# Hybrid decoder layer on one core: the last two row tiles share one attention-times-values visit, and output products move between scores and transposes

## The chip, the cores and the metric

The kernel runs on one core of a Trainium2 chip. The metric is the device time of one execution in microseconds, here the median of three runs. It is written directly against the engines: each engine has its own program, and semaphores order them.

## What is computed

The reference is one decoder layer over 512 tokens of width 1024, in float32:

```
h = x @ w_in                       # one projection, split into q,k,v,gates,indexer,latents
o_a = dsa(qa, ka, va, iq, ik, iw) * silu(ga)    # branch A: each query attends to its top-128 keys, 8 heads of 64
o_b = mla(c_q, c_kv, k_rope, ...) * silu(gb)    # branch B: causal latent attention, 8 heads of 64 (+32 rotary)
out = concat(o_a, o_b) @ w_out
x   = layernorm(alpha * x + out) * ln_g + ln_b
```

## The kernel before, in words

Tokens are cut into four row tiles of 128 (TT = 4), which are taken in the order 3, 2, 1, 0 (`ORDER`), so that the causal length falls: a query tile has 4, 3, 2 and then 1 key tiles. "Tile 0" below is the first that is taken and "tile 3" the last, with one key tile.

After the projections TensorE runs a pipeline over 64 units u. Units 0 to 31 are branch A, units 32 to 63 are branch B: eight heads for each row tile, so tile 2 of branch B is units 48 to 55 and tile 3 is units 56 to 63. For one unit of branch B:

- TensorE makes the scores (`scores`, L1335) into one of two PSUM banks.
- VectorE masks them into `probs` and takes the row maximum (`mask_unit`, L996).
- ScalarE takes the exponential (`exp_unit`, L752).
- VectorE divides by the row sum, two units later (`normalise_b`, L1033 and L1035).
- TensorE transposes the result three units later (`transposes`, L1368), and ScalarE copies it out of PSUM (`copy_probsT`, L771).
- Once per row tile, five units after its last head, TensorE multiplies all eight heads with the values (`outputs`, L1406; called a visit below). The result is gated by VectorE (`gate_obT`, L1044).

The gated result of a row tile is `oT`, in halves: half 0 is branch A (k = 0 to 3), half 1 is branch B (k = 4 to 7). Each half is split for precision: ScalarE rounds it to a high part (`copy_oT_hi`, L782), and VectorE or GpSimd subtracts that to get the low part (`oT_low`, L386). The output projection (`out_products`, L1445) takes high times high, high times low weights, and low times high: 48 products of 128x512 for a row tile (the last tile has three column pieces of 512, 256 and 256 instead of two of 512, so 24 products of 512 and 48 of 256). They are handed out a few per unit as filler. VectorE then does the layer norm: `ln_residual` (L1055 and L1060) reads the output bank and thereby frees it, then `ln_stats`, `ln_centre` (L1071), `ln_scale` (L1078). GpSimd takes the root of the variance (L614). SyncE stores.

Every engine works through its own list in the order in which the code is written. The lists of ScalarE and VectorE that matter here, for unit u:

```
ScalarE: copy_probsT(u-3); copy_oT_hi(i-1, 0) if u is 48+4 or 56+4 ...; exp_unit(u); ...
VectorE: normalise_b(u-2); mask_unit(u); oT_low(V, i-1, 0) and gate_obT(i-1) if u%8 == 4; layer norm pieces
```

The layer norm pieces of tile 0 stand at units 53 to 57 and those of tile 1 at units 61 to 65. The output banks of tiles 0 to 2 are the same two, so the first product of a tile waits (`out_ps_read`) for the `ln_residual` of the tile before.

Of the kernel before, what the change touches and what calls it, by code (L numbers as in the profile page):

```python
# [6 lines left out]
P = 128  # L7
# [19 lines left out]
def build(nc, x, xT, positions, pos_row, freqs, w_in, q_norm_g, w_uq, kv_norm_g, w_ukv, w_out, ln_g, ln_b, out):  # L27
# [98 lines left out]
    for u in range(NU):  # L126
        slots.append(u)
        for i in range(TT):
            if u == G_AFTER[i]:
                slots.append((i,))  # L130
    OUT_AT = [NU_A + HEADS * (i + 1) + OT_AT + 2 for i in range(TT)]

    PIECES = [[slice(0, BANK), slice(BANK, D_MODEL)]] * (TT - 1) + [[slice(0, BANK), slice(BANK, BANK + BANK // 2),
# [56 lines left out]
    qaT = sb("qaT", 162, [P, A_HEADS, SEQ], f32r)  # L190
    oT1 = sb("oT1", 24, [P, 2, KT, P], f32r)
    probsT_b = [sb(f"probsT_b{j}", kib, [P, BANK]) for j, kib in enumerate((162, 164, 166, 168, 170, 172, 174, 176, 88, 90, 196, 198))]

    probs = sb("probs", 16, [P, NPROBS, BANK])
    trig_tmp = sb("trig_tmp", 178, [P, 2, TT * FREQ_B])
# [36 lines left out]
    with ExitStack() as ctx:  # L232
# [125 lines left out]
        def copy_free(eng, u):  # L358

            if u < NU_A:  # L360
                if last_user(u) is not None:
                    eng.wait_ge(pv_done, HEADS * (last_user(u) // HEADS + 1))
                return probsT[u][:, :]
            if u >= NU_A + len(probsT_b):
                eng.wait_ge(pv_done, HEADS * ((u - len(probsT_b)) // HEADS + 1))
            return probsT_b[(u - NU_A) % len(probsT_b)][:, 0:unit(u)[3]]

        def oT_src(i, b):

# [10 lines left out]
        def oT_low(eng, i, b):  # L380

            dst = (oT0, oT1)[i % 2]
            eng.wait_ge(oT_hi_ready, 2 * i + b + 1)
            if i + b > 0:
                eng.wait_ge(oT_lo_ready, 2 * i + b)
            eng.tensor_tensor(dst[:, 1, 4 * b:4 * b + 4, :], oT_src(i, b), dst[:, 0, 4 * b:4 * b + 4, :],  # L386
                              ALU.subtract).then_inc(oT_lo_ready, 1)

        def out_steps(i):


            halves = ((0, KT // 2), (KT // 2, KT))
            blocks = [(b, h) for h in halves for b in range(len(PIECES[i]))] if i < TT - 1 else \
                     [(b, h) for b in range(len(PIECES[i])) for h in halves]
            return [(b, k, j) for b, (k0, k1) in blocks for low in (False, True)
                    for k in range(k0, k1) for j in ((2,) if low else (0, 1))]

# [103 lines left out]
        def _(pool):  # L501
# [112 lines left out]
                pool.tensor_tensor(rstd, aggr[:, 2:3], minus_half[:, 0:1], ALU.pow).then_inc(rstd_ready, 1)  # L614


            for i in range(TT):
                if i < TT - 1:
                    oT_low(pool, i, 1)
                if i == 1:  # L620
                    root(0)
            root(1)
            root(2)
            root(3)


        @block.scalar
        def _(act):
# [161 lines left out]
            for u in range(NU + T_LAG):  # L790
                for w in turned_at(u):
                    if not by_dve(w):
                        copy_probsT(w)
                i, j = divmod(u - NU_A, HEADS)
                if 1 < i < TT and j == OT_AT:
                    copy_oT_hi(i - 1, 0)
                if 2 <= u < NU:
                    exp_unit(u)
                if u in VB_AT:
                    copy_vb(VB_AT.index(u))  # L800
                if u == O_FIRST:
                    copy_oT_hi(0, 0)
                for t in range(TT):
                    if u == TURN_AT[t]:
                        turn_gate(t)
                if 0 < i < TT and j == OT_AT + 1:
                    copy_oT_hi(i - 1, 1)
            copy_oT_hi(TT - 1, 0)
            copy_oT_hi(TT - 1, 1)


# [1 line left out]
        def _(dve):  # L813
# [274 lines left out]
            for u in range(NU):  # L1088
                if u - NORM_LAG >= NU_A:
                    normalise_b(u - NORM_LAG)  # L1090
                if u >= 2:
                    mask_unit(u)
                for w in turned_at(u):
                    if by_dve(w):
                        copy_probsT(w)
                v, j = divmod(u, HEADS)
                i = v - TT
                if u in (BLOCK_UNITS + 2, NU_A + 2):
                    row_sums_a(u // BLOCK_UNITS - 1)
                for t in range(TT):  # L1100
                    if u == GATE_AT[t]:
                        gate_oaT(t)
                for n in range(TT):
                    if u == PET_AT[n]:
                        qpe_blocks(n)
                if 1 < i and j == OT_AT:
                    oT_low(V, i - 1, 0)
                if 0 < i and j == OT_AT:
                    gate_obT(i - 1)
                for t in range(TT - 2):  # L1110
                    for at_u, take in ln_schedule(t):
                        if at_u == u:
                            take()
# [23 lines left out]
        def _(pe):  # L1137
# [233 lines left out]
            def outputs(u):  # L1371
# [21 lines left out]
                                    ins.then_inc(pv_done, 1)  # L1393
                    return

                i = v - TT
                if h < HEADS - 1:
                    return
                pe.wait_ge(*((o_ps_read, TURN_RANK.index(A_RANK[i]) + 1) if i < 2 else (ob_ps_read, i - 1)))
                for w in range(u - HEADS + 1, u, 2):  # L1400
                    for a in range(2):
                        wait_copied(pe, w + a)
                    h = unit(w)[2]
                    for j in range(m + 1):
                        for a in range(2):
                            ins = mm(ps_o[A_DIM * a:A_DIM * (a + 1), i % 2, h // 2 * P:(h // 2 + 1) * P],  # L1406
                                     vb[:, j, (h + a) * V_DIM:(h + a + 1) * V_DIM],
                                     probsT_b[(w + a - NU_A) % len(probsT_b)][:, j * P:(j + 1) * P], start=(j == 0), stop=(j == m))
                            if j == m:
                                ins.then_inc(pv_done, 1)  # L1410

# [9 lines left out]
            def out_products(i, a, z):  # L1421
# [3 lines left out]
                for n in range(a, z):  # L1425
                    b, k, j = steps[n]
                    first, final = n == steps.index((b, 0, 0)), n == steps.index((b, KT - 1, 2))
                    cols = PIECES[i][b]
                    half, wcols = cols.start // BANK, slice(cols.start % BANK, cols.start % BANK + cols.stop - cols.start)
                    if b == 0 and j in (0, 2) and k in (0, KT // 2):  # L1430
                        pe.wait_ge((oT_hi_ready, None, oT_lo_ready)[j], 2 * i + 1 + (k > 0))
# [20 lines left out]
            for u in range(NU + PV_LAG):  # L1452
                if 2 <= u < NU:
                    scores(u)
                for w in turned_at(u):
                    transposes(w)
                if u in VB_AT:
# [7 lines left out]
                i, j = divmod(u - NU_A, HEADS)  # L1465
# [3 lines left out]
                if 0 <= u - A_HALF_AT < 8:  # L1469
                    out_products(0, 3 * (u - A_HALF_AT), 3 * (u - A_HALF_AT + 1))  # L1470
                if 0 <= u - OUT_AT[0] - 2 < 6:
                    out_products(0, 3 * KT + 4 * (u - OUT_AT[0] - 2), 3 * KT + 4 * (u - OUT_AT[0] - 1))
                for t in range(1, TT - 1):
                    if 0 <= u - OUT_AT[t] < HEADS:
                        out_products(t, per * (u - OUT_AT[t]), per * (u - OUT_AT[t] + 1))
# [66 lines left out]
```

## Time and profile before

| | |
|---|---|
| median of 3 runs | 291.01 us (290.87 to 291.7) |
| profiled execution, its own time | 291.71 us |
| its span in the trace | 289.9 us |
| TensorE busy | 281.6 us, 97% of the span |
| VectorE busy | 234.3 us, 81% |
| ScalarE busy | 148.4 us, 51% |
| GpSimd busy | 168.2 us, 58% |
| TensorE granted clock over the span | 0.995 |

A matmul that follows another starts before the modelled end of the first, so the time that one costs is the distance between starts and not its own duration. Times inside the trace are counted from the start of the span.

### The profile page before, as it was taken

Reading aid. Unit: us, or ns where it says so; the run is one execution under the profiler, and the core shown is the slowest. Engines: PE = TensorE matmul, PEld = TensorE weight load, DVE = VectorE, ACT = ScalarE, POOL = GpSimd, SP = SyncE. Lnnn points to the kernel's source line nnn. Section 1 sums busy time; section 2 is a strip of 40 time slices with the busy share of each in tenths; the row PEclk is TensorE's granted clock in tenths of the full one; section 3 lists DMA queues with packets and bytes.
Section 4 is the critical chain, followed back from the end, with each engine's and each line's share of the span. In section 5 each row is a group of like instructions: output and inputs, shape, how many; then the busy total and the mean of one; then the engine's idle time right before and its main releaser. Section 6 shows DMA issues by size and latency. Waiting matters only on the chain.

```text
span 289.9 us, 5157 instructions
## 1 busy us (share of the span) xinstructions
PE 281.6 (97%) x1696; PEld 234.8 (81%) x1696; DVE 234.3 (81%) x536; ACT 148.4 (51%) x351; POOL 168.2 (58%) x174
## 2 busy tenths in 40 slices
PE   8999999999999999999999999999999999999990
PEld 8999987778888888888888887885778788887890
DVE  2799498889999999999984788668894759786755
ACT  4765353585433367224188696677773744432000
POOL 5698956333089999999946999632990102011101
PEclk9999999999999999999999999999999999999997
DMA  7966662222604297221238667507800000400412
GB/s 229 350 195 187 179 176 72 75 72 67 153 4 142 72 222 216 72 72 38 72 102 196 222 144 235 123 2 280 300 2 2 0 3 1 145 2 5 142 72 72
DMA packets 20074, 34.20 MB, mean 118 GB/s; under 512 B 6640, under 2 KB 9200, under 8 KB 19792
## 3 DMA queue, kind: packets, MB, share of 16 engines
q1 hardware_dynamic: 19616, 33.71, 39.3%
q8 instruction: 14, 0.23, 0.3%
q10 hardware_dynamic: 432, 0.16, 0.3%
q14 instruction: 12, 0.10, 0.1%
HBM read 26.52 MB, written 2.10 MB: 99 GB/s over the span
## 4 chain that ended last, share of the span: by engine, by line
PE 96%; DVE 2%; issue 1%; DVEq 0%; POOL 0%; POOLq 0%
PE ps L1143 52%; PE ps L1445 16%; PE ps L1368 6%; PE ps L1335 6%; PE ps L1406 3%; PE ps L1389 3%; PE ps L1158 2%; PE ps L1325 2%; PE ps L1328 2%; PE ps L1278 1%; PE ps L1252 1%; PE ps L1418 1%; DVE y_last L1071 1%; PE ps L1261 0%; PE ps L1235 0%
## 5 line engine op out<-in xcount | busy, mean ns | idle before, releaser
L533 POOL TENSOR_TENSOR w_lo<-w_raw,w_hi 128x512 fp32r<-128x512 f32 (+3 forms) x62 | 82.8, 1355 | 26.7 <-ACT w_hi L645 26.0
L645 ACT ACTIVATE w_hi<-w_raw 128x512 fp32r<-128x512 f32 (+3 forms) x62 | 36.0, 589 | 57.7 <-PE ps L1143 55.7
L752 ACT ACTIVATE probs<-probs,small 128x512 f32<-128x512 f32 (+3 forms) x64 | 35.7, 558 | 18.6 <-DVE small L996 18.3
L1143 PE MATMUL ps<-w_hi,x_lo 128*128 128x512 f32 (+2 forms) x128 | 45.0, 356 | 0.0
L1445 PE MATMUL ps<-wo_hi,oT 128*128 128x512 f32 (+1 forms) x144 | 44.9, 383 | 0.0
L1143 PE MATMUL ps<-w_lo,x_hi 128*128 128x512 f32 (+2 forms) x128 | 44.9, 356 | 0.0
L1143 PE MATMUL ps<-x_hi,w_hi 128*128 128x512 f32 x96 | 38.1, 396 | 0.0
L1143 PE MATMUL ps<-x_hi,w_lo 128*128 128x512 f32 x96 | 37.4, 390 | 0.0
L1143 PE MATMUL ps<-x_lo,w_hi 128*128 128x512 f32 x96 | 37.4, 390 | 0.0
L1143 PE MATMUL ps<-w_hi,x_hi 128*128 128x512 f32 (+1 forms) x92 | 34.8, 378 | 0.0
L1445 PEld LDWEIGHTS ps<-wo_hi,oT 128*128 128x128 f32 x144 | 25.9, 189 | 4.0 <-issue 0.5
L1368 PE MATMUL ps<-ident,probs 128*128 128x128 f32 x160 | 28.6, 276 | 0.3
L1368 PEld LDWEIGHTS ps<-ident,probs 128*128 128x128 f32 x160 | 19.5, 140 | 10.8 <-issue 6.2
L1143 PEld LDWEIGHTS ps<-w_hi,x_lo 128*128 128x128 f32 x128 | 24.1, 188 | 2.5
L1143 PEld LDWEIGHTS ps<-w_lo,x_hi 128*128 128x128 f32 x128 | 24.1, 188 | 2.5
L953 DVE MATCH_REPLACE8 score<-small,score 128x256 f32<-128x256 f32 (+2 forms) x48 | 25.5, 541 | 0.0
L996 DVE CUSTOM_DVE_ANT_0 probs<-ps,causal 128x128 f32<-128x128 f32 (+3 forms) x40 | 17.8, 446 | 9.4 <-PE ps L1335 8.0
L386 POOL TENSOR_TENSOR oT<-gate,oT 128x512 fp32r<-128x512 f32 x4 | 5.1, 1284 | 34.2 <-ACT oT L782 34.2
L950 DVE MAX8 small<-score 128x8 f32<-128x256 f32 (+2 forms) x48 | 23.5, 544 | 0.0
L1335 PE MATMUL ps<-kbT,qbT 96*128 96x512 f32 (+3 forms) x64 | 22.6, 434 | 0.0
L1143 PEld LDWEIGHTS ps<-x_hi,w_hi 128*128 128x128 f32 x96 | 18.0, 188 | 4.9 <-ACT w_hi L645 0.7
L771 ACT ACTIVATE probsT_b<-ps 128x512 f32<-128x512 f32 (+3 forms) x32 | 13.8, 432 | 15.8 <-PE ps L1368 15.6
(163 smaller groups left out, 606.5 us busy)
## 6 DMA issues: line engine op xcount, KB each, us to landing
w_raw<-in_w_in SPq DMA_DIRECT2D x20, 512.0 KB, 3.7
kaT_swap<-kaT SPq DMA_DIRECT2D x8, 256.0 KB, 3.8
w_raw<-in_w_out SPq DMA_DIRECT2D x4, 512.0 KB, 4.2
wo_early<-in_w_out SPq DMA_DIRECT2D x4, 512.0 KB, 3.7
wo_raw_b<-in_w_out SPq DMA_DIRECT2D x4, 512.0 KB, 5.2
x_res<-in_x SPq DMA_DIRECT2D x4, 512.0 KB, 7.0
x_raw<-in_xT SPq DMA_DIRECT2D x3, 512.0 KB, 7.3
out_y<-y SPq DMA_DIRECT2D x6, 256.0 KB, 2.1
```

The costliest lines, as they stand in the source:

```text
L533: pool.tensor_tensor(w_lo[:, s, 0:n], w_raw[:, s, 0:n], w_hi[:, s, 0:n], ALU.subtract).then_inc(w_lo_ready, 1)
L645: act.activation(dst, w_raw[:, s, 0:n], ACT.Copy).then_inc(w_hi_ready, 1)
L752: act.activation(probs[:, u % NPROBS, 0:N], probs[:, u % NPROBS, 0:N], ACT.Exp, bias=neg_max[:, u % 8:u % 8 + 1], scale=-1.0, accum_out=ro ...
L771: act.activation(dst, ps_pT[:, slot_of[u] % 2, 0:N], ACT.Copy).then_inc(probsT_copied, 1)
L950: step(V.max(top8[:, 8 * j:8 * j + 8], sc))
L953: step(V.match_replace(out=sc, in_to_replace=top8[:, 8 * j:8 * j + 8], in_values=sc, imm_value=TAKEN))
L996: V.tensor_tensor_reduce(out=probs[:, u % NPROBS, 0:N], in0=ps_s[:, u % 2, 0:N], in1=bias, scale=-scale, scalar=3.0e38, op0=ALU.add, op1=A ...
L1143: ins = mm(dst, a, b, start=start and j == 0, stop=stop and j == len(pairs) - 1)
L1335: ins = mm(ps_s[:, b, 0:N], qbT[:, h, t], kbT[:, h, 0:N], start=True, stop=True)
L1368: ins = nc.tensor.transpose(bank[:, j * P:(j + 1) * P], probs[:, u % NPROBS, j * P:(j + 1) * P], ident[:, :])
L1389: ins = mm(oa_bank(v)[A_DIM * a:A_DIM * (a + 1), h // 2 * P:(h // 2 + 1) * P], va[:, j, (h + a) * A_DIM:(h + a + 1) * A_DIM], probsT[w + 2 ...
L1445: ins = mm(out_ps(i, b), oT[i % 2][:, o, k, :], w[:, wcols], start=first, stop=final)
```

## The change

Three things are done together.

1. Inside each unit TensorE's output products stand between the scores and the transposes; before, they stood after the transposes, the visit and the gate transposes.
2. The visit of tile 2 (units 48 to 55, made at unit 60) is put off to unit 68 and made with that of tile 3. Their transposed probabilities get their own buffers (`short_b`), in space that is free by then.
3. The output products of tile 2 in units 62 to 67 are now four per unit and only its first half (24 products). After the common visit come 12 products of tile 3 (half 0, first piece), then tile 2's other 24, then tile 3's remaining 60. Tile 3's products go by halves first and pieces second. The gating, the high part and the low part of tile 2's half 1 move to the end of the lists of VectorE and ScalarE, and its low part from GpSimd to VectorE.

```diff
+    SPLIT_ORDER = [(0, 0), (0, 1), (1, 0), (1, 1), (2, 0), (3, 0), (2, 1), (3, 1)]
...
+    short_b = [sb(f"short_b{n}", kib, [P, unit(NU - 2 * HEADS + n)[3]]) for n, kib in
+               enumerate([170 + n for n in range(HEADS)] + [88 + n / 2 for n in range(HEADS)])]
...
-            blocks = [(b, h) for h in halves for b in range(len(PIECES[i]))] if i < TT - 1 else \
-                     [(b, h) for b in range(len(PIECES[i])) for h in halves]
+            blocks = [(b, h) for h in halves for b in range(len(PIECES[i]))]
...
             # GpSimd
+            for i in range(TT - 2):
+                oT_low(pool, i, 1)
             for i in range(TT):
-                if i < TT - 1:
-                    oT_low(pool, i, 1)
-                if i == 1:
-                    root(0)
-            root(1)
...
             # ScalarE
-                if 0 < i < TT and j == OT_AT + 1:
+                if 0 < i < TT - 1 and j == OT_AT + 1:
                     copy_oT_hi(i - 1, 1)
-            copy_oT_hi(TT - 1, 0)
+                if u == NU:
+                    copy_oT_hi(TT - 1, 0)
+            copy_oT_hi(TT - 2, 1)
             copy_oT_hi(TT - 1, 1)
...
             # VectorE
-                if 0 < i and j == OT_AT:
+                if 0 < i < TT - 1 and j == OT_AT:
                     gate_obT(i - 1)
...
-            gate_obT(TT - 1)
-            oT_low(V, TT - 1, 1)
+            for t in range(TT - 2, TT):
+                gate_obT(t)
+            for t in range(TT - 2, TT):
+                oT_low(V, t, 1)
...
             # TensorE, outputs
-                if h < HEADS - 1:
+                if h < HEADS - 1 or v == NPASS - 2:
                     return
...
             # TensorE, the loop over units
                 if 2 <= u < NU:
                     scores(u)
+                if 0 <= u - A_HALF_AT < 8:
+                    out_products(0, 3 * (u - A_HALF_AT), 3 * (u - A_HALF_AT + 1))
+                if 0 <= u - OUT_AT[0] - 2 < 6:
+                    out_products(0, 3 * KT + 4 * (u - OUT_AT[0] - 2), 3 * KT + 4 * (u - OUT_AT[0] - 1))
+                if 0 <= u - OUT_AT[1] < HEADS:
+                    out_products(1, per * (u - OUT_AT[1]), per * (u - OUT_AT[1] + 1))
+                if 0 <= u - OUT_AT[2] < 6:
+                    out_products(2, 4 * (u - OUT_AT[2]), 4 * (u - OUT_AT[2] + 1))
                 for w in turned_at(u):
                     transposes(w)
...
-            done = per * (NU + PV_LAG - OUT_AT[TT - 2])
-            out_products(TT - 2, done, NSTEP)
-            out_products(TT - 1, 0, 3 * KT * len(PIECES[TT - 1]))
+            last_first, last_all = 3 * KT // 2, 3 * KT * len(PIECES[TT - 1])
+            out_products(TT - 1, 0, last_first)
+            out_products(TT - 2, NSTEP // 2, NSTEP)
+            out_products(TT - 1, last_first, last_all)
```

TensorE's list at units 61 and 62, before. L1335 is `scores`, L1368 `transposes`, L1445 `out_products`; oT_97 belongs to tiles 1 and 3, oT_68 to tiles 0 and 2:

```order
L1335 MATMUL ps<-kbT,qbT 128x128
L1368 MATMUL ps<-ident,probs 128x128
L1445 MATMUL ps<-wo_hi,oT_97 128x512
L1445 MATMUL ps<-wo_lo_b,oT_97 128x512
L1445 MATMUL ps<-wo_hi,oT_97 128x512 x4
L1335 MATMUL ps<-kbT,qbT 128x128
L1368 MATMUL ps<-ident,probs 128x128
L1445 MATMUL ps<-wo_hi,oT_68 128x512
L1445 MATMUL ps<-wo_lo_a,oT_68 128x512
```

The same place in the changed kernel (L1349 is `scores`, L1382 `transposes`, L1461 `out_products`):

```order
L1349 MATMUL ps<-kbT,qbT 128x128
L1461 MATMUL ps<-wo_hi,oT_97 128x512
L1461 MATMUL ps<-wo_lo_b,oT_97 128x512
L1461 MATMUL ps<-wo_hi,oT_97 128x512 x4
L1382 MATMUL ps<-ident,probs 128x128
L1349 MATMUL ps<-kbT,qbT 128x128
L1461 MATMUL ps<-wo_hi,oT_68 128x512
L1461 MATMUL ps<-wo_lo_a,oT_68 128x512
```

The transpose of a unit now stands behind all its products, and the first product of tile 2 directly behind the scores of unit 62.

ScalarE's list at the end, before. L752 is the exponential, L771 the copy of a transposed unit, L782 the high part of an oT half:

```order
L771 ACTIVATE probsT_b_99<-ps 128x128
L782 ACTIVATE oT_68<-gate 128x512
L752 ACTIVATE probs,small<-probs,small 128x128
L771 ACTIVATE probsT_b_100<-ps 128x128
L752 ACTIVATE probs,small<-probs,small 128x128
L782 ACTIVATE oT_68<-gate 128x512
L771 ACTIVATE probsT_b_101<-ps 128x128
```

The same place in the changed kernel (L781 the copy, L792 the high part, L762 the exponential):

```order
L781 ACTIVATE short_b_119<-ps 128x128
L792 ACTIVATE oT_68<-gate 128x512
L762 ACTIVATE probs,small<-probs,small 128x128
L781 ACTIVATE short_b_120<-ps 128x128
L762 ACTIVATE probs,small<-probs,small 128x128
L781 ACTIVATE short_b_121<-ps 128x128
```

The high part of tile 2's half 0 (the first oT_68) still stands behind the copy of unit 57's transpose. The high part of its half 1 has left this place.

## Rows read from the trace of the kernel before

**Rows 1.** The page: busy time by engine, and the ending chain by engine.

```profile
PE 281.6 (97%) x1696; PEld 234.8 (81%) x1696; DVE 234.3 (81%) x536; ACT 148.4 (51%) x351; POOL 168.2 (58%) x174
...
PE 96%; DVE 2%; issue 1%; DVEq 0%; POOL 0%; POOLq 0%
```

**Rows 2.** The chain that ended last: start, us, what.

```profile
268.78 14.15 PE ps L1445 x84
```

**Rows 3.** Timeline, TensorE, unit 41: start us, us, engine, line, operation.

```profile
211.75 0.81 PE L1335 MATMUL ps<-kbT,qbT 96*128 96x384 f32 x2
212.53 0.63 PE L1368 MATMUL ps<-ident,probs 128*128 128x128 f32 x4
```

**Rows 4.** Timeline, TensorE, units 58 to 62.

```profile
248.74 0.39 PE L1335 MATMUL ps<-kbT,qbT 96*128 96x128 f32 x2
249.16 0.41 PE L1368 MATMUL ps<-ident,probs 128*128 128x128 f32 x2
...
252.52 0.38 PE L1335 MATMUL ps<-kbT,qbT 96*128 96x128 f32 x2
252.74 0.27 PE L1368 MATMUL ps<-ident,probs 128*128 128x128 f32 x1
252.95 1.97 PE L1406 MATMUL ps<-probsT_b,vb 128*64 128x128 f32 x32
...
256.33 0.39 PE L1335 MATMUL ps<-kbT,qbT 96*128 96x128 f32 x2
...
258.05 0.39 PE L1335 MATMUL ps<-kbT,qbT 96*128 96x128 f32 x2
```

**Rows 5.** Timeline, ScalarE, unit 60.

```profile
253.05 0.28 ACT L771 ACTIVATE probsT_b<-ps 128x128 f32<-128x128 f32 x1 [1.00 <-PE ps L1368]
253.23 0.62 ACT L782 ACTIVATE oT<-gate 128x512 fp32r<-128x512 f32 x1
```

**Rows 6.** Timeline, VectorE, units 60 to 63.

```profile
253.88 0.69 DVE L386 TENSOR_TENSOR oT<-gate,oT 128x512 fp32r<-128x512 f32 x1 [0.64 <-ACT oT L782]
...
256.97 0.68 DVE L1055 SCALAR_TENSOR_TENSOR y<-x_res,ps 128x512 f32<-128x512 f32 x1
...
258.30 0.15 DVE L1033 RECIPROCAL small<-small 128x1 f32<-128x1 f32 x1
258.48 1.07 DVE L1035 TENSOR_SCALAR probs<-probs,small 128x128 f32<-128x128 f32 x1
...
261.19 0.28 DVE L1035 TENSOR_SCALAR probs<-probs,small 128x128 f32<-128x128 f32 x1
261.39 0.28 DVE L996 CUSTOM_DVE_ANT_0 probs<-ps,causal 128x128 f32<-128x128 f32 x1
261.60 0.08 DVE L996 DVE_READ_ACCUMULATOR2_ANT small<- 128x1 f32 x1
...
262.57 0.16 DVE L1033 RECIPROCAL small<-small 128x1 f32<-128x1 f32 x1
```

**Rows 7.** Timeline, TensorE, unit 64.

```profile
261.62 0.30 PE L1368 MATMUL ps<-ident,probs 128*128 128x128 f32 x1
```

**Rows 8.** Timeline, GpSimd, around unit 62.

```profile
258.19 1.29 POOL L386 TENSOR_TENSOR oT<-gate,oT 128x512 fp32r<-128x512 f32 x1 [11.26 <-ACT oT L782]
```

**Rows 9.** Timeline, VectorE, units 52 and 53.

```profile
238.35 0.69 DVE L1044 TENSOR_TENSOR gate<-ps,gate 128x512 f32<-128x512 f32 x1 [1.18 <-PE ps L1406]
...
239.15 0.35 DVE L1035 TENSOR_SCALAR probs<-probs,small 128x256 f32<-128x256 f32 x1
239.87 0.42 DVE L996 CUSTOM_DVE_ANT_0 probs<-ps,causal 128x256 f32<-128x256 f32 x1 [0.37 <-PE ps L1335]
...
240.22 0.68 DVE L1055 SCALAR_TENSOR_TENSOR y<-x_res,ps 128x512 f32<-128x512 f32 x1
```

**Rows 10.** Timeline, TensorE, the two products that follow the scores of unit 1.

```profile
162.77 0.45 PE L1143 MATMUL ps<-latT_hi,w_hi 128*128 128x512 f32 x1
163.06 0.39 PE L1143 MATMUL ps<-latT_lo,w_hi 128*128 128x512 f32 x1
```

More of the change, by code:

```diff
@@ L363, in copy_free, with probsT_of @@
                 return probsT[u][:, :]
-            if u >= NU_A + len(probsT_b):
+            if u >= NU - 2 * HEADS:
+                eng.wait_ge(pv_done, HEADS * (u // HEADS - 1))
+            elif u >= NU_A + len(probsT_b):
                 eng.wait_ge(pv_done, HEADS * ((u - len(probsT_b)) // HEADS + 1))
-            return probsT_b[(u - NU_A) % len(probsT_b)][:, 0:unit(u)[3]]
+            return probsT_of(u)
+        def probsT_of(u):
+            n = u - (NU - 2 * HEADS)
+            return short_b[n][:, :] if n >= 0 else probsT_b[(u - NU_A) % len(probsT_b)][:, 0:unit(u)[3]]
         def oT_src(i, b):
@@ L382, in oT_low @@
             dst = (oT0, oT1)[i % 2]
-            eng.wait_ge(oT_hi_ready, 2 * i + b + 1)
-            if i + b > 0:
-                eng.wait_ge(oT_lo_ready, 2 * i + b)
+            n = SPLIT_ORDER.index((i, b))
+            eng.wait_ge(oT_hi_ready, n + 1)
+            if n > 0:
+                eng.wait_ge(oT_lo_ready, n)
             eng.tensor_tensor(dst[:, 1, 4 * b:4 * b + 4, :], oT_src(i, b), dst[:, 0, 4 * b:4 * b + 4, :],
@@ L614, in root @@
                 pool.tensor_tensor(rstd, aggr[:, 2:3], minus_half[:, 0:1], ALU.pow).then_inc(rstd_ready, 1)
+            for i in range(TT - 2):
+                oT_low(pool, i, 1)
             for i in range(TT):
-                if i < TT - 1:
-                    oT_low(pool, i, 1)
-                if i == 1:
-                    root(0)
-            root(1)
-            root(2)
-            root(3)
+                root(i)
         @block.scalar
@@ L1394, in outputs @@
                     return
-                i = v - TT
-                if h < HEADS - 1:
+                if h < HEADS - 1 or v == NPASS - 2:
                     return
-                pe.wait_ge(*((o_ps_read, TURN_RANK.index(A_RANK[i]) + 1) if i < 2 else (ob_ps_read, i - 1)))
-                for w in range(u - HEADS + 1, u, 2):
+                for w in range(u - (2 * HEADS if v == NPASS - 1 else HEADS) + 1, u, 2):
+                    v, m, h, N = unit(w)
+                    i = v - TT
+                    if h == 0:
+                        pe.wait_ge(*((o_ps_read, TURN_RANK.index(A_RANK[i]) + 1) if i < 2 else (ob_ps_read, i - 1)))
                     for a in range(2):
                         wait_copied(pe, w + a)
-                    h = unit(w)[2]
                     for j in range(m + 1):
@@ L1407, in outputs @@
                                      vb[:, j, (h + a) * V_DIM:(h + a + 1) * V_DIM],
-                                     probsT_b[(w + a - NU_A) % len(probsT_b)][:, j * P:(j + 1) * P], start=(j == 0), stop=(j == m))
+                                     probsT_of(w + a)[:, j * P:(j + 1) * P], start=(j == 0), stop=(j == m))
                             if j == m:
@@ L1430, in out_products @@
                     if b == 0 and j in (0, 2) and k in (0, KT // 2):
-                        pe.wait_ge((oT_hi_ready, None, oT_lo_ready)[j], 2 * i + 1 + (k > 0))
+                        pe.wait_ge((oT_hi_ready, None, oT_lo_ready)[j], SPLIT_ORDER.index((i, int(k > 0))) + 1)
                     if i == 0 and n in (0, 3 * KT):
@@ L1464, in _ @@
                     outputs(u - PV_LAG)
-                i, j = divmod(u - NU_A, HEADS)
                 for t in range(1, TT):
@@ L1468, in _ @@
                         gate_transposes(t)
[L1469 to L1475, printed above, removed]
-            done = per * (NU + PV_LAG - OUT_AT[TT - 2])
-            out_products(TT - 2, done, NSTEP)
-            out_products(TT - 1, 0, 3 * KT * len(PIECES[TT - 1]))
+            last_first, last_all = 3 * KT // 2, 3 * KT * len(PIECES[TT - 1])
+            out_products(TT - 1, 0, last_first)
+            out_products(TT - 2, NSTEP // 2, NSTEP)
+            out_products(TT - 1, last_first, last_all)
 NWARM = 9
```

## The prediction

> **What bounds the kernel now.** I read the page first, then the chain that ended last, then the timelines of the last 80 us engine by engine. TensorE is busy 97% of the span and is 96% of the chain [rows 1]. Behind the last visit it runs 84 products without a gap, to 282.93 [rows 2]; the span ends 7.0 us later with the layer norm of the last tile and its store. So nothing gets shorter unless TensorE does less, waits less, or that tail changes. The change removes no product. Its gain can only come from TensorE's waits in units 40 to 68, and any new wait there is paid in full, because behind it there is no slack until the end.
>
> How a wait is seen: the distance from one start to the next against what the work takes. The scores of one key tile take 0.22 us (252.52 to 252.74), and a unit with one key tile and six products takes 1.72 (256.33 to 258.05) [rows 4]. So six products with one transpose take 1.50; a transpose is 0.11 of that and a product 0.23. In unit 58 the transposes start 0.42 after the scores instead of 0.22 [rows 4], and in unit 41, with three key tiles, 0.78 after them instead of 0.66 [rows 3]: VectorE had not finished the division.
>
> **Output products ahead of the transposes: the gain.** In each unit a transpose now gets 0.7 to 1.4 us more before it can be late. Unit 58 saves 0.20 and unit 41 0.12. Two more units (40 and 56) show smaller excesses of the same kind, for which I estimate the mean of these two rows, 0.16 each at most; half of that is my value, so 0.5 us together, between 0.32 and 0.64. In unit 64 the transpose starts at 261.62 [rows 7] where two units of 1.72 behind 258.05 would put it at 261.49: 0.13 of wait, which goes or is replaced (below). Gain so far 0.6.
>
> **The common visit.** Unit 60 lasts 3.81 and a unit without a visit 1.72, so the visit costs 2.09 for products whose own group lasts 1.97 [rows 4]. The products remain; one entry and one exit go. The bounds are 0.1 and 0.3 (the 0.21 between transpose and visit instead of 0.11, and as much again at the exit); I take 0.15.
>
> **What is queued behind the later transposes: the loss.** ScalarE's list has, for unit 60: copy of transpose 57, high part of tile 2's half 0, exponential. Before, transpose 57 started at 252.74, its copy at 253.05, the high part at 253.23, and VectorE's low part at 253.88 [rows 4 to 6], so 1.14 behind the transpose. In the changed kernel the transpose stands behind six products, and these steps come later with it. VectorE's next instruction after the mask of unit 60 is that low part. It idles there some 2 us, although the input of the high part has been ready since branch A. Behind the low part wait, in this order: division of unit 59, mask 61, `ln_residual` of tile 1's first piece, and it is this last one that frees the bank for tile 2's first product.
>
> Call X the start of transpose 57. On VectorE:
> - the low part starts at X+1.14. A gating of the same form plus a reciprocal takes 0.80 (238.35 to 239.15) [rows 9], less 0.18 for the reciprocal (258.30 to 258.48) [rows 6]: 0.62;
> - a division of one key tile takes 0.18 + 0.20 (261.19 to 261.39), about 0.39, and a mask 0.21 (261.39 to 261.60) [rows 6];
> - so `ln_residual` starts at X+2.35, lasts 0.68 [rows 6] and reaches TensorE 0.12 later, at X+3.15. The 0.12 is the way from a division to a transpose (0.15 from 261.47 to 261.62, of which TensorE's load is a part) [rows 6, 7].
>
> On TensorE without a wait: transpose 0.11, unit 61 with 1.72, scores of unit 62 with 0.22: X+2.05. Before, the first product of tile 2 stood behind the transpose too and the residual at 256.97 was over by 257.65, while the scores came at 258.05 [rows 4, 6]: it had 0.6 us to spare. Now TensorE waits **1.1 us**.
>
> From there units 62 to 66 have four products, not six: 1.26 with scores, 1.04 without. TensorE reaches transpose 61 at X+6.4. VectorE: residual and statistics take 1.33 (256.97 to 258.30), then division 60, mask 62, another 1.33, division 61. This ends at X+2.35+1.33+0.60+1.33+0.39 = X+6.0: in time. Then mask 63, 0.21, and aggregate and centring, 0.97 (261.60 to 262.57) [rows 6], and division 62 ends at X+7.65, at TensorE X+7.8. Transpose 62 could start at X+7.5: **0.3 us** more of wait. Transpose 63 is in time.
>
> Here a neighbour matters. The division of unit 60 took 1.07 instead of 0.28 while GpSimd's low part of 1.29 us ran [rows 6, 8]. The change moves this to the end of VectorE's list, and I count division 60 at 0.39. If it stayed slow, 0.8 more would fall on VectorE's stretch, and some 0.4 on transpose 61. The Trainium skill (SBUF — State Buffer, Who interferes with whom) says that VectorE and GpSimd share one pair of ports under an exclusive lock; by that rule the slow division goes with its neighbour, and the trace agrees (1.07 beside, 0.28 apart).
>
> The same wait exists one tile earlier, smaller. Tile 1's first product in unit 54 needs tile 0's residual, which stands in unit 53 behind the gating at 238.35. Gating and reciprocal bring the division to 239.15, this gives way after 0.27 (0.35 less the overlap of 0.08), mask 0.35 (239.87 to 240.22), residual 0.68, signal 0.12 [rows 9]: 2.22 behind the gating. TensorE leaves the visit 0.14 before the gating starts and, by the prices above, needs 0.44 for scores, 0.92 for four products, 0.25 for two transposes and 0.44 for scores: 2.05, so 1.91 behind the gating. It waits **0.3**, where before the transposes and four products between visit and scores covered it.
>
> **A boundary that the trace hardly shows.** Scores now precede a product. After the scores of unit 1 two products lie 0.29 apart instead of 0.23 [rows 10]: at most 0.06 for each of 24 units, 1.4 us. Against that, transposes no longer precede products. Unit 61 shows no loss at that boundary (1.72 = 0.22 + 0.11 + 6 x 0.23). I take nothing, since the second pass of scores is as long as a transpose, and keep 1.4 for the upper end.
>
> **The last stretch.** GpSimd's roots no longer stand behind a low part, which nobody waits for, and SyncE's list is the same. Behind the common visit, 12 products of tile 3 (2.7 us) and the visit's last third (1 us) cover the gating (0.69), the high part (0.62) and the low part (0.69) of tile 2's half 1. VectorE has tile 2's layer norm, about 5.5 us, after tile 2's last product at +8.2; tile 3's first piece is complete at +13.8 and its second 1.44 before the last. Residual and statistics of that piece take 0.9. So the tail of 7.0 us is unchanged; if this cover failed it would cost up to 0.5.
>
> The Trainium skill (TensorE: Matmul & The Clock Gate, Architectural detail) states that ScalarE and VectorE work strictly first in, first out. By it the high part cannot pass the copy that waits, which is what this forecast needs. The row agrees in order (253.05, then 253.23), but no run here has yet shown it with the input waiting. If ScalarE could pass it, the 1.1 would vanish, as in the second rival.
>
> **Sum.** +1.1 +0.3 +0.3 -0.6 -0.15 = +0.95, taken as +0.9. The profiled execution took 291.71 for a span of 289.9, that is 1.8 outside it, and would give 292.6; it lies 0.7 above the median of 291.01, to which I add the same 0.9: **291.9 us**.
>
> **Rivals.**
> - *Waits as above (49 in 100):* 291.9, own range 291.2 to 292.6. It falls on both sides of the bound.
> - *The waits are small (16 in 100):* only 0.3 to 0.5 at tile 2's first product, since some step of the VectorE chain is quicker: 291.0 to 291.2, no change.
> - *The cover is complete (14 in 100):* this is the other side. If the residual of tile 1 is done by X+2.05, none of the three waits appears and the gains of 0.6 and 0.15 stay, up to 0.9 with their upper bounds: 290.1, faster. It decides at 1.1 us in the VectorE chain between low part and residual. For it speaks that VectorE idles 2 us there; against it, that the idle time is ahead of the chain and not in it.
> - *The boundary costs (21 in 100):* half to all of 1.4 on top of 0.9: 292.6 to 293.3, slower. For it the one row with 0.29, against it that there the weights differ.
>
> **How the numbers follow.** A measurement tells this kernel from no change at about 0.3%, 0.9 us (290.14 and 291.88). Faster: the third case, 0.14. Same: the second and half of the first, 0.16 + 0.24 = 0.40. Slower: the other half and the fourth, 0.46. The range goes down into the third case, to 290.3, and up into the fourth, to 292.9.
>
> **What would show it.** In the changed trace: transposes of units 41, 56 and 58 without excess; one visit of 48 products; VectorE idle some 2 us before the low part in unit 60; TensorE's first product of tile 2 about 1.1 late behind the scores of unit 62 and the first of tile 1 0.3 late in unit 54; transpose 62 late by 0.3; the tail of 7.0 unchanged. Wrong would be: no gap at those two products (then faster), gaps of more than 0.02 behind every score (then slower), or a wait of tile 2's half 1 behind the visit.

## The result, and the profile after

The changed kernel takes 292.05 us (median of 11 runs, 291.48 to 292.45) against 291.10 for the kernel before (11 runs beside it, 290.87 to 291.70). The ratio is 1.0026, 95% interval 1.0017 to 1.0036: slower by 0.76 us, between 0.5 and 1.05. The two medians lie further apart, 0.95, but inside that interval. The forecast was 291.9, 0.9 more than before.

The page of the changed kernel: its span, the busy time by engine as in [rows 1], and the row of the output products:

```profile
span 290.3 us, 5157 instructions
PE 279.9 (96%) x1696; PEld 233.3 (80%) x1696; DVE 231.9 (80%) x537; ACT 148.6 (51%) x351; POOL 167.3 (58%) x173
...
L1461 PE MATMUL ps<-wo_hi,oT 128*128 128x512 f32 (+1 forms) x144 | 46.8, 398 | 1.1 <-DVE y L1067 1.0
```

TensorE has 1.7 us less busy time. The last row has what takes its place: the output products (L1461) had idle time of 1.1 us before them, and 1.0 of it ended with VectorE's residual (L1067). That idle time was 0.0 before.

Spans also differ at their beginnings, where the kernels are the same. So I measure the part that the change touches by itself: from the first scores of unit 40, the first with three key tiles, to the last residual of the last tile. The kernel before (timelines of TensorE and VectorE):

```profile
209.88 0.81 PE L1335 MATMUL ps<-kbT,qbT 96*128 96x384 f32 x2
...
282.95 0.42 DVE L1055 SCALAR_TENSOR_TENSOR y_last<-x_res,ps 128x256 f32<-128x256 f32 x1 [1.99 <-PE ps L1445]
```

The changed kernel (timeline of TensorE; its last residual, at 283.31, is shown further down):

```profile
209.62 0.81 PE L1349 MATMUL ps<-kbT,qbT 96*128 96x384 f32 x2
```

Before, the stretch takes 73.07 us; in the changed kernel it takes 73.69, or 0.62 more.

TensorE in the changed kernel, units 60 to 65 (timeline; start us, us, engine, line, operation, idle time before it):

```profile
253.55 0.27 PE L1382 MATMUL ps<-ident,probs 128*128 128x128 f32 x1
253.66 0.38 PE L1349 MATMUL ps<-kbT,qbT 96*128 96x128 f32 x2
253.80 0.48 PE L1461 MATMUL ps<-wo_hi,oT 128*128 128x512 f32 x1
254.12 0.40 PE L1461 MATMUL ps<-wo_lo_b,oT 128*128 128x512 f32 x1
...
255.38 0.39 PE L1349 MATMUL ps<-kbT,qbT 96*128 96x128 f32 x2
256.73 0.47 PE L1461 MATMUL ps<-wo_hi,oT 128*128 128x512 f32 x1 [0.96 <-DVE y L1067]
257.04 0.39 PE L1461 MATMUL ps<-wo_lo_a,oT 128*128 128x512 f32 x1
...
258.99 0.27 PE L1382 MATMUL ps<-ident,probs 128*128 128x128 f32 x1
...
260.03 0.27 PE L1382 MATMUL ps<-ident,probs 128*128 128x128 f32 x1
...
261.34 0.30 PE L1382 MATMUL ps<-ident,probs 128*128 128x128 f32 x1
...
263.53 2.84 PE L1422 MATMUL ps<-short_b,vb 128*64 128x128 f32 x48
```

Unit 61 takes 1.72 (253.66 to 255.38), as before [rows 4]: a product behind scores costs nothing extra. From the start of the scores to that of the second product behind them is 0.46 in unit 61 (253.66 to 254.12) and 1.66 in unit 62 (255.38 to 257.04): tile 2's first product has waited 1.20. The trace puts a product's start early where it follows scores without a wait, so I measure such waits to the second product. Two transposes with four products between them are 1.04 apart when nothing waits (258.99 to 260.03); transpose 62 follows after 1.31, 0.27 late. The visit is one, of 48 products.

ScalarE's timeline of the changed kernel at the same place:

```profile
253.86 0.28 ACT L781 ACTIVATE short_b<-ps 128x128 f32<-128x128 f32 x1 [1.05 <-PE ps L1382]
254.03 0.62 ACT L792 ACTIVATE oT<-gate 128x512 fp32r<-128x512 f32 x1
254.56 0.39 ACT L762 ACTIVATE probs<-probs,small 128x128 f32<-128x128 f32 x1
```

VectorE's timeline of the changed kernel:

```profile
252.37 0.29 DVE L1008 CUSTOM_DVE_ANT_0 probs<-ps,causal 128x128 f32<-128x128 f32 x1 [0.65 <-PE ps L1349]
...
254.69 0.69 DVE L401 TENSOR_TENSOR oT<-gate,oT 128x512 fp32r<-128x512 f32 x1 [2.02 <-ACT oT L792]
255.30 0.15 DVE L1045 RECIPROCAL small<-small 128x1 f32<-128x1 f32 x1
...
255.90 0.68 DVE L1067 SCALAR_TENSOR_TENSOR y<-x_res,ps 128x512 f32<-128x512 f32 x1
```

ScalarE stood idle for 1.05 at the copy of transpose 57, although the high part behind it reads a tile that branch A had finished long before; VectorE stood idle for 2.02 at the low part. With X = 253.55, the start of transpose 57, the low part starts at X+1.14 and the residual at X+2.35, the two numbers of the prediction.

The chain that ended last in the changed kernel leaves TensorE at this one place of the stretch (start, us, what): it runs through the high part, the low part and the residual to tile 2's first products.

```profile
254.03 0.63 ACT oT L792
254.69 0.69 DVE oT L401
255.99 0.61 DVE y L1067
256.73 1.16 PE ps L1461 x4
```

One tile earlier, in unit 54, the same on a smaller scale (TensorE's timeline of the changed kernel again):

```profile
240.37 0.60 PE L1349 MATMUL ps<-kbT,qbT 96*128 96x256 f32 x2
241.06 0.47 PE L1461 MATMUL ps<-wo_hi,oT 128*128 128x512 f32 x1
241.37 0.39 PE L1461 MATMUL ps<-wo_lo_a,oT 128*128 128x512 f32 x1
...
242.74 0.60 PE L1349 MATMUL ps<-kbT,qbT 96*128 96x256 f32 x2
242.99 0.58 PE L1461 MATMUL ps<-wo_hi,oT 128*128 128x512 f32 x1
243.41 0.40 PE L1461 MATMUL ps<-wo_lo_a,oT 128*128 128x512 f32 x1
```

From the scores to the second product is 1.00 (240.37 to 241.37), and 0.67 in unit 55 (242.74 to 243.41): 0.33 of wait. In units 40 to 52 and in units 56 and 58 no transpose is late any more. Taken as the length of the whole unit, that saves 0.09, 0.16, 0.17 and 0.23 in units 40, 41, 56 and 58. From the scores of unit 54 to those of unit 60 TensorE needs 11.58 (240.37 to 251.95) although this wait is in it; before it needed 11.70 (240.82 to 252.52).

The tail is the same: the last residual starts at 283.31 and the span ends 7.0 later (VectorE's timeline of the changed kernel):

```profile
282.34 0.43 DVE L1072 BATCH_NORM_STATS2 small<-y_last 128x6 f32<-128x256 f32 x1
283.31 0.42 DVE L1067 SCALAR_TENSOR_TENSOR y_last<-x_res,ps 128x256 f32<-128x256 f32 x1 [0.54 <-PE ps L1461]
```

VectorE still has 0.54 to spare ahead of the last residual, against 1.99 before: the new order of the end has used up most of this margin, but not all of it.

### The profile page after: what moved, and what is told of

It reads as the page before. It is cut to its first block, busy times and chain, and to the rows that moved or that the text cites. A ratio compares the mean times of both kernels' runs of the same rounds, so it can differ in the third digit from the quotient of the medians.

```text
span 290.3 us, 5157 instructions
## 1 busy us (share of the span) xinstructions
PE 279.9 (96%) x1696; PEld 233.3 (80%) x1696; DVE 231.9 (80%) x537; ACT 148.6 (51%) x351; POOL 167.3 (58%) x173
## 4 chain that ended last, share of the span: by engine, by line
PE 93%; DVE 2%; DMA 2%; issue 1%; ACT 0%; DVEq 0%; SPq 0%; ACTq 0%
PE ps L1157 52%; PE ps L1461 15%; PE ps L1382 6%; PE ps L1349 6%; PE ps L1403 3%; PE ps L1422 3%; PE ps L1339 2%; PE ps L1172 2%; DMA w_raw<-in_w_in 2%; PE ps L1342 2%; PE ps L1266 1%; PE ps L1434 1%; DVE y_last L1083 1%; PE ps L1275 0%; PE ps L1249 0%
## 5 line engine op out<-in xcount | busy, mean ns | idle before, releaser
L1461 PE MATMUL ps<-wo_hi,oT 128*128 128x512 f32 (+1 forms) x144 | 46.8, 398 | 1.1 <-DVE y L1067 1.0
L762 ACT ACTIVATE probs<-probs,small 128x512 f32<-128x512 f32 (+3 forms) x64 | 35.6, 556 | 10.8 <-DVE small L1008 10.4
L1461 PEld LDWEIGHTS ps<-wo_hi,oT 128*128 128x128 f32 x144 | 26.0, 189 | 6.9 <-issue 1.8
L1382 PE MATMUL ps<-ident,probs 128*128 128x128 f32 x160 | 28.4, 275 | 0.4
L1382 PEld LDWEIGHTS ps<-ident,probs 128*128 128x128 f32 x160 | 19.8, 140 | 9.3 <-issue 4.8
L628 POOL TENSOR_TENSOR small<-small 128x1 f32<-128x1 f32 x4 | 4.1, 1018 | 38.4 <-DVE small L1077 38.4
L1349 PE MATMUL ps<-kbT,qbT 96*128 96x512 f32 (+3 forms) x64 | 22.8, 436 | 0.0
L1157 PEld LDWEIGHTS ps<-x_lo,w_hi 128*128 128x128 f32 x96 | 18.0, 188 | 3.8
```

What stands on the lines that cost most here:

```text
L762: act.activation(probs[:, u % NPROBS, 0:N], probs[:, u % NPROBS, 0:N], ACT.Exp, bias=neg_max[:, u % 8:u % 8 + 1], scale=-1.0, accum_out=ro ...
L1157: ins = mm(dst, a, b, start=start and j == 0, stop=stop and j == len(pairs) - 1)
L1349: ins = mm(ps_s[:, b, 0:N], qbT[:, h, t], kbT[:, h, 0:N], start=True, stop=True)
L1382: ins = nc.tensor.transpose(bank[:, j * P:(j + 1) * P], probs[:, u % NPROBS, j * P:(j + 1) * P], ident[:, :])
```

## The experiments

My theory is that of the prediction: TensorE pays at tile 2's first product because the work that frees its bank stands on VectorE behind a low part, which stands on ScalarE behind the copy of a transpose that the change has put later. The main rivals are that a product behind scores costs something each time, and that VectorE has too much work there, whatever it waits for. Each kernel was timed 5 to 12 times, beside the kernel before; the latter's median was 291.10 beside the change, 291.40 beside the first four of the experiments below, and 291.32 beside the others (visit split, two visits, high part later, both cures). So compare ratios, not medians.

| kernel | median | ratio to before, interval | unit 40 to last residual, against before |
|---|---|---|---|
| the change | 292.05 | 1.0026, 1.0017 to 1.0036 | +0.62 |
| products first only | 290.78 | 0.9985, 0.9977 to 0.9994 | -0.32 |
| common visit only | 291.57 | 1.0008, 0.9997 to 1.0019 | +0.47 |
| change, high part first | 290.51 | 0.9974, 0.9965 to 0.9983 | -0.69 |
| change, residual first | 290.34 | 0.9968, 0.9956 to 0.9979 | -1.03 |
| change, visit split | 292.60 | 1.0041, 1.0027 to 1.0056 | +1.01 |
| products first, residual first, two visits | 290.71 | 0.9975, 0.9963 to 0.9987 | -0.85 |
| change, high part later | 292.15 | 1.0033, 1.0021 to 1.0044 | +1.06 |
| change, both cures | 290.23 | 0.9964, 0.9952 to 0.9977 | -1.18 |

The last column comes from one profiled execution of each. It is the finer of the two for waits in this stretch: where two kernels have the same work and no different wait, as from unit 40 to unit 52, their traces agree to 0.02 (24.60 to 24.62 in eight of the nine, 24.82 with the products behind the transposes). It lies inside the interval of the ratio (of 291, 0.001 is 0.3 us) in every row.

**One half of the change: products first only.** The kernel before, with its product calls moved up, between the scores and the transposes of the loop:

```diff
+                if 0 <= u - A_HALF_AT < 8:
+                    out_products(0, 3 * (u - A_HALF_AT), 3 * (u - A_HALF_AT + 1))
+                if 0 <= u - OUT_AT[0] - 2 < 6:
+                    out_products(0, 3 * KT + 4 * (u - OUT_AT[0] - 2), 3 * KT + 4 * (u - OUT_AT[0] - 1))
+                for t in range(1, TT - 1):
+                    if 0 <= u - OUT_AT[t] < HEADS:
+                        out_products(t, per * (u - OUT_AT[t]), per * (u - OUT_AT[t] + 1))
...
-                if 0 <= u - A_HALF_AT < 8:
-                    out_products(0, 3 * (u - A_HALF_AT), 3 * (u - A_HALF_AT + 1))
...
```

> The kernel before with one part of the change: output products between scores and transposes. My theory (waits moved along ScalarE's and VectorE's lists): the late transposes of units 41, 56 and 58, 64 and 65 are covered (-0.7 in all against the kernel before), tile 1's first product in unit 54 waits 0.25, and tile 2's first product in unit 62 waits at most 0.1, because the visit still stands in unit 60 and gives VectorE its 2 us. Sum -0.4 +- 0.2. Rival (a product behind scores costs something every time, 0.03 to 0.06 in 24 units): 0.3 to 0.7 slower than before.

It is 0.44 us faster by the ratio, so the rival is out. The same hold on VectorE is there, but TensorE has its visit of 32 products to do meanwhile (this kernel's timeline of TensorE, then of VectorE):

```profile
254.05 0.27 PE L1368 MATMUL ps<-ident,probs 128*128 128x128 f32 x1
254.25 1.97 PE L1406 MATMUL ps<-probsT_b,vb 128*64 128x128 f32 x32
256.15 0.49 PE L1335 MATMUL ps<-kbT,qbT 96*128 96x128 f32 x2
...
257.97 0.39 PE L1335 MATMUL ps<-kbT,qbT 96*128 96x128 f32 x2
258.33 0.47 PE L1445 MATMUL ps<-wo_hi,oT 128*128 128x512 f32 x1
258.64 0.40 PE L1445 MATMUL ps<-wo_lo_a,oT 128*128 128x512 f32 x1
```

VectorE:

```profile
255.18 0.69 DVE L386 TENSOR_TENSOR oT<-gate,oT 128x512 fp32r<-128x512 f32 x1 [2.02 <-ACT oT L782]
```

Idle 2.02 on VectorE, as in the changed kernel, but from the scores to the second product is 0.67 (257.97 to 258.64), where 0.46 is taken when nothing waits: a wait of 0.21 instead of 1.20. The expectation had at most 0.1. VectorE even has more to do here: with the visit it also gates tile 2, and its residual comes 2.32 behind the low part (at 257.50), not 1.21. But TensorE has 2.09 more of its own in between: from transpose 57 to the scores of unit 62 it takes 3.92 (254.05 to 257.97), against 1.83 in the changed kernel (253.55 to 255.38). So the two halves of the change work against each other: the first makes VectorE late, and the second takes away the visit that hid it.

**The other half: common visit only.** The changed kernel with the products back behind the transposes.

> The changed kernel with the output products back behind the transposes and the visit, so only the common visit and the new order of the end. My theory: one visit less saves 0.35 to 0.4 (each has a fixed part), the short units 62 to 66 have VectorE late for transposes 61 and 62, 0.4 and 0.5 instead of 0.13 and 0.04, and tile 2's first product does not wait. Sum +0.35 against the kernel before. Rival (the common visit and the short units carry the whole loss): +0.8 or more.

This kernel's timeline of TensorE, the transposes of units 60, 61 and 62:

```profile
256.87 0.27 PE L1382 MATMUL ps<-ident,probs 128*128 128x128 f32 x1
...
258.38 0.30 PE L1382 MATMUL ps<-ident,probs 128*128 128x128 f32 x1 [0.31 <-DVE probs L1047]
...
259.96 0.30 PE L1382 MATMUL ps<-ident,probs 128*128 128x128 f32 x1 [0.35 <-DVE probs L1047]
```

Transposes 61 and 62 are 1.51 and 1.58 behind their predecessors instead of 1.04: 0.47 and 0.54 late. In all, transpose 63 comes 4.15 behind transpose 60 where 3.12 would do, 1.03 late; before, it was 0.23 late (260.00 to 264.72, 4.72, where 4.49 is enough in the run with two visits and no wait). That is 0.80 more, and with 0.33 for the visit saved (measured further down) it gives the 0.47 of the table. By the ratio it is +0.23, and its interval includes no change and +0.5, but not the rival's 0.8. By the trace the parts alone make -0.32 and +0.47, +0.15 in all, where both together make +0.62: the other 0.47 is the price of their meeting.

**The place on ScalarE: high part first.** In the changed kernel:

```diff
+                i, j = divmod(u - NU_A, HEADS)
+                if 1 < i < TT and j == OT_AT:
+                    copy_oT_hi(i - 1, 0)
                 for w in turned_at(u):
                     if not by_dve(w):
                         copy_probsT(w)
-                i, j = divmod(u - NU_A, HEADS)
-                if 1 < i < TT and j == OT_AT:
-                    copy_oT_hi(i - 1, 0)
```

> The changed kernel with one edit on ScalarE: in units 52 and 60 the high part of the next tile's half 0 stands ahead of the copy of a transpose and not behind it. My theory (this place in the list holds VectorE for 2 us): VectorE's low part in unit 60 starts 1.2 earlier, tile 2's first product no longer waits (1.13 in the changed kernel), transpose 62 no longer waits (0.28), tile 1's first product still waits 0.26. Against the changed kernel -1.4, against the kernel before -0.7 to -0.8. Rival (VectorE has too much work there, whatever it waits for): less than 0.4 is recovered.

This kernel's timeline of VectorE:

```profile
253.03 0.69 DVE L401 TENSOR_TENSOR oT<-gate,oT 128x512 fp32r<-128x512 f32 x1 [0.69 <-ACT oT L792]
...
254.24 0.68 DVE L1067 SCALAR_TENSOR_TENSOR y<-x_res,ps 128x512 f32<-128x512 f32 x1
```

VectorE's idle time falls from 2.02 to 0.69 and the residual is over before TensorE asks for the bank. In the timeline of TensorE unit 62 has no wait, transpose 62 is 0.13 late and the wait of unit 54 stands. The kernel is 0.76 us faster than the one before by the ratio, 1.31 less than the changed kernel by the trace (1.4 expected; the wait of 1.20 and half of transpose 62's lateness are 1.34). The rival that VectorE simply has too much to do would have left at least 1.0 of it.

**The place on VectorE: residual first.** In the changed kernel, with ScalarE as it was:

```diff
+                for t in range(TT - 2):
+                    if u == OUT_AT[t] + 6:
+                        ln_residual(t, 0)
                 if 1 < i and j == OT_AT:
                     oT_low(V, i - 1, 0)
...
-                return [(u + 7, lambda: ln_residual(t, 0)), (u + 8, lambda: ln_residual(t, 1)), (u + 9, lambda: ln_stats(t)),
+                return [(u + 8, lambda: ln_residual(t, 1)), (u + 9, lambda: ln_stats(t)),
```

> The changed kernel with one edit on VectorE: the first residual of tiles 0 and 1 (which frees an output bank) stands in units 52 and 60 ahead of the low part and not one unit later behind a division and a mask. ScalarE's list is as in the changed kernel. My theory: both waits for the bank go (0.26 in unit 54, 1.13 in unit 62), and the work behind the low part is 1.3 shorter, so transpose 62 is in time too. VectorE still idles at the low part, but only 0.7. Against the changed kernel -1.7, against the kernel before -1.0. Rival (it is the idle time of VectorE that costs, not which work stands behind it): as slow as the changed kernel or -0.3.

This kernel's timeline of VectorE:

```profile
251.86 0.68 DVE L1067 SCALAR_TENSOR_TENSOR y<-x_res,ps 128x512 f32<-128x512 f32 x1
252.57 0.69 DVE L1072 BATCH_NORM_STATS2 small<-y 128x6 f32<-128x512 f32 x1
253.96 0.69 DVE L401 TENSOR_TENSOR oT<-gate,oT 128x512 fp32r<-128x512 f32 x1 [0.69 <-ACT oT L792]
```

The residual and its statistics fill 1.33 of the time in which VectorE stood idle, and the bank is free 2 us before it is asked for. This gives 0.93 by the ratio and 1.65 against the changed kernel by the trace (1.7 expected; 1.20, 0.33 and 0.13 of transpose 62's lateness are 1.66). One thing I had wrong: transpose 62 is still 0.14 late.

**More of the suspected cause: high part later.** In the changed kernel the high part stands behind the exponential as well:

```diff
-                if 1 < i < TT and j == OT_AT:
-                    copy_oT_hi(i - 1, 0)
                 if 2 <= u < NU:
                     exp_unit(u)
+                if 1 < i < TT and j == OT_AT:
+                    copy_oT_hi(i - 1, 0)
```

> The changed kernel with the suspected wait made longer: in units 52 and 60 the high part stands behind the exponential too. My theory: VectorE's low part of unit 60 starts later by what the exponential takes on ScalarE, 0.5, and tile 2's first product is later by the same 0.5, as is all behind it; unit 54 is unchanged. +0.5 against the changed kernel, +1.1 to 1.3 against the kernel before. Rival (the wait is set by VectorE's own work): no change against the changed kernel.

This kernel's timeline of TensorE:

```profile
255.10 0.39 PE L1349 MATMUL ps<-kbT,qbT 96*128 96x128 f32 x2
256.83 0.47 PE L1461 MATMUL ps<-wo_hi,oT 128*128 128x512 f32 x1 [1.35 <-DVE y L1067]
257.14 0.39 PE L1461 MATMUL ps<-wo_lo_a,oT 128*128 128x512 f32 x1
```

And of VectorE:

```profile
254.79 0.69 DVE L401 TENSOR_TENSOR oT<-gate,oT 128x512 fp32r<-128x512 f32 x1 [2.41 <-ACT oT L792]
```

VectorE idles for 2.41, 0.39 more, and TensorE waits 1.58 (255.10 to 257.14 less 0.46), 0.38 more than in the changed kernel: the wait follows the place of the high part one for one. The exponential holds ScalarE for 0.39 and not 0.5. By the trace the whole stretch is 0.44 longer, by the ratio 1.0033 against 1.0026, whose intervals overlap; here the trace decides.

**The price of a visit: visit split.** The changed kernel, with its common visit cut in two:

```diff
-            def outputs(u):
+            def outputs(u, ws=None):
...
-                for w in range(u - (2 * HEADS if v == NPASS - 1 else HEADS) + 1, u, 2):
+                for w in range(*ws) if ws else range(u - HEADS + 1, u, 2):
...
-                if u - PV_LAG >= NU_A:
+                if u - PV_LAG == NU - 1:
+                    outputs(NU - 1, (NU - 2 * HEADS, NU - HEADS, 2))
+                elif u - PV_LAG >= NU_A:
                     outputs(u - PV_LAG)
...
             out_products(TT - 1, 0, last_first)
+            outputs(NU - 1, (NU - HEADS, NU, 2))
```

> The changed kernel with the common visit cut in two again, at the end: tile 2's 32 products, then the 12 output products of tile 3, then tile 3's 16 visit products, then the rest. No new wait for data: gating and parts of tile 2 are ready 1.5 behind the second visit, and its low part is wanted 1.8 behind it. My theory (a visit has a fixed part of about 0.35: an entry, a first stretch and an exit at a change from one kind of product to the other): +0.35 against the changed kernel, +1.0 to 1.1 against the kernel before. Rival (the common visit saves only 0.15, as the prediction had it): +0.15 against the changed kernel.

This kernel's timeline of TensorE, its two visits and what follows each:

```profile
263.00 1.97 PE L1422 MATMUL ps<-short_b,vb 128*64 128x128 f32 x32
264.89 0.50 PE L1461 MATMUL ps<-wo_hi,oT 128*128 128x512 f32 x1
...
267.88 1.09 PE L1422 MATMUL ps<-short_b,vb 128*64 128x128 f32 x16
268.90 0.50 PE L1461 MATMUL ps<-wo_hi,oT 128*128 128x512 f32 x1
```

The stretch is 0.39 longer than in the changed kernel, and the ratio 0.0015 higher. The inside of the visits shows where a part of it sits: 32 products take 1.89 from start to exit (263.00 to 264.89) and 16 take 1.02, so 16 more products cost 0.87 and a visit of any size 0.15 besides. The first two products behind a visit are 0.34 apart and not 0.23 (268.90 to 269.24), and in the kernel before a visit starts 0.21 behind a transpose and not 0.11 [rows 4]. That makes 0.36 with entry and exit. Why a visit costs this, no run shows.

**The same price once more, and all waits gone.** The kernel before with products first and residual first (visits separate), and the changed kernel with both cures:

> The kernel before with the output products ahead of the transposes and the first residuals in units 52 and 60, visits separate as before. My theory: all waits of TensorE in units 40 to 66 go, so the covered transposes give 0.7 and nothing is lost: -0.7 against the kernel before, and 0.3 to 0.4 above the kernel with the residual first and a common visit. Rival (the common visit brings nothing once the waits are gone): equal to that kernel, -1.0.

> The changed kernel with both cures: high part ahead of the copy on ScalarE, and the first residual ahead of the low part on VectorE. My theory: no wait of TensorE is left after the second cure alone, so the first adds nothing: within 0.2 of that kernel, -1.0 against the kernel before. Rival (some of the late transposes still cost something in it): 0.3 or more faster than the residual-first kernel.

Neither has a wait of TensorE at a product or a transpose in units 53 to 66. By the trace they are 0.33 apart (-0.85 and -1.18), which is the visit again; by the ratios, 0.9975 and 0.9964, the intervals overlap. The new order of the end (the third part of the change) is in only one of the two, and it leaves no difference beyond the visit's. Against the kernel with the residual first alone the distance is 0.18 and not 0.3 to 0.4, since that one has transpose 62 late. The kernel with both cures is the fastest by the trace, 290.23 us, 1.05 faster than the kernel before (interval 0.7 to 1.4) and some 1.8 faster than the changed one. It is 0.15 faster by the trace than the one with the residual first alone, and that is the 0.14 of transpose 62 left there.

## Why the prediction was right

Term by term, against what the traces show:

| term | predicted | measured in the changed kernel |
|---|---|---|
| late transposes covered, units 40 to 65 | -0.6 | -0.87: 0.19 to unit 52, 0.45 from unit 54 to 60, 0.23 in units 64 to 66 |
| one visit less | -0.15 | -0.33 to -0.39 |
| tile 2's first product waits | +1.1 | +1.20 |
| transpose 62 waits | +0.3 | +0.27 |
| tile 1's first product waits | +0.3 | +0.33 |
| sum | +0.9 | +0.6 by the trace, +0.76 by the ratio |

**The waits.** All three came where they were placed, with their sizes to 0.1. The edits at unit 60 on ScalarE and on VectorE each remove the large one, and the one that makes the hold longer makes it longer by as much. What the walk along the lists had right was which work stands behind which: the residual that frees a bank is nowhere near the transposes in the code, and it is what paid.

**The visit** is the term that was mis-sized. I took 0.15 from a busy time of 1.97 against 2.09 of elapsed time, but a matmul's own time in the trace overlaps with its successor's start, so 1.97 had part of the exit in it. Read by starts, the group takes 1.89. I also took the products themselves for unchanged, but 0.15 of fixed price lies inside the group. The whole is more than twice what I took: splitting a visit costs 0.39, joining two gives 0.33 where nothing waits.

**The covered transposes** gave 0.87 and not 0.6: the start of a late transpose shows a little less than the unit's length (0.20 and 0.23 in unit 58), of the two units that I had only estimated I took half, and unit 56 was worth 0.17, more than unit 41; and units 65 and 66 had 0.10 behind the 0.13 of unit 64. Both errors go the same way, the wait 0.1 the other, and the 0.9 came out 0.14 above the ratio and 0.3 above the trace.

**Luck.** That 291.9 is only 0.15 from the median of 292.05 is in part luck: the kernel before ran 0.1 slower than in the three runs that I had, and the medians lie further apart than the ratio puts them. Nor could the total tell much. The range, 290.3 to 292.9, holds every median of the table but one. The prediction's bound between no change and slower, 0.9 us, lies within the interval from 0.5 to 1.05, so the time does not decide between the two; its interval only excludes that nothing changed. What bears the account are the terms in the trace and the edits that remove them.

**The neighbour on GpSimd.** With the low part of tile 2's half 1 gone from GpSimd, the division of unit 60 took 0.29, as counted. No run put it back in the changed kernel, so its price there is not shown. Other traces show the hold itself. In the run with products first, residual first and two visits, GpSimd's low part runs from 258.70 to 259.98; the division that starts in it, at 259.39, takes 0.67 and ends at 260.06. In the kernel before it ends at 259.55, with GpSimd's at 259.48 [rows 6, 8]. With products first only, the division starts 0.42 ahead of GpSimd's low part (259.01 and 259.43) and takes 0.29. So the slow one is a division that starts while GpSimd's low part runs, and it ends just behind it.

**The rivals.** That the boundary between scores and products costs something is refuted by unit 61 (1.72 before and after) and by the kernel with products first only. The complete cover, the faster rival, did not come by itself, but it was one small edit away: residual first gives it but for the 0.14 of transpose 62, and both cures give all of it.

**First in, first out.** The prediction had no row with a ready instruction held behind a waiting one. The changed kernel has it: 1.05 of idle time on ScalarE at the copy with the high part behind it. That the high part was ready is shown by the run with high part first, where it starts at 252.38, before transpose 57 at 253.23. The trace agrees with the Trainium skill (TensorE: Matmul & The Clock Gate, Architectural detail), by which ScalarE and VectorE are strictly first in, first out.

## What to carry to other kernels

When an instruction is moved later on the bounding engine, follow its result through the other engines' lists: whatever stands behind its consumer there moves too, even work whose inputs were ready. Look above all for the instruction that frees a buffer of the bounding engine, and put it ahead of anything that can wait. Two edits can cost more together than the sum of what each costs alone, when one removes the work that hid the other's delay, so test them apart.

## What the runs showed that I had not expected

- A visit, 16 to 48 small float32 products between two runs of output products, has a fixed price of 0.33 to 0.39 us, of which some 0.15 lie inside it. It goes with the number of visits and not with the work in them. Changing the order of scores, transposes and output products has no such price (unit 61 is 1.72 in both orders).
- 2.0 us of idle time on VectorE, at the same instruction, cost 1.20 us in one kernel and 0.21 in the other. What decided was not the idle time but what each engine still had to do behind it: with the separate visit 2.09 more on TensorE, against 1.11 more on VectorE.
